# A hybrid encoder step on one core: the prologue's modulation pieces, squares and engine orders rearranged

## What is computed

```python
sh1, sc1, gt1, sh2, sc2, gt2 = adaln(cs[grp], w_ada[i], b_ada[i])   # silu(c) @ w_ada + b_ada, split in six
h = modulate(rms_norm(x, norm_mix[i]), sh1, sc1)                    # norm * (1 + scale) + shift
mix, S_fin = gla_mixer(h, S0, gla_w_in[j], ...)                     # begins with h @ gla_w_in
```

## Time and profile before

| | us |
|---|---|
| median of 3 executions (lowest, highest) | 1425.83 (1424.13, 1426.85) |
| the profiled execution | 1425.07 |
| its span in the trace | 1423.1 |
| TensorE busy | 1383.6 (97%) |
| VectorE, ScalarE, GpSimd busy | 950.0, 653.9, 88.4 |

### The profile page before, as it was taken

The page is one execution under the profiler, slowest core; times in us unless marked ns, Lnnn a source line. Parts: engine busy times, 40 slices in busy tenths (PEclk is TensorE's granted clock), DMA queues, the critical chain, the costliest instruction groups (busy, mean ns, idle before and its releaser), DMA issues.

```text
span 1423.1 us, 26319 instructions
## 1 busy us (share of the span) xinstructions
PE 1383.6 (97%) x10896; PEld 1304.1 (92%) x10896; DVE 950.0 (67%) x1591; ACT 653.9 (46%) x1454; POOL 88.4 (6%) x149
## 2 busy tenths in 40 slices
PE   8999999999999999999899999999899999999999
PEld 6878887989999999999898787879799999999999
DVE  4678677368988788778665556475888654554544
ACT  4543344256554254252465555643565552552530
POOL 0000000110000000000300000000300000000000
PEclk9999999999999999999999999999999999999999
DMA  9543533234444544535433233212334223223222
GB/s 383 221 156 138 184 131 105 67 119 161 157 155 143 175 150 148 175 119 166 155 132 104 77 104 132 80 38 83 119 119 149 90 67 112 89 67 112 75 64 106
DMA packets 37582, 182.42 MB, mean 128 GB/s; under 512 B 4246, under 2 KB 6422, under 8 KB 26072
## 3 DMA queue, kind: packets, MB, share of 16 engines
q1 hardware_dynamic: 22552, 126.98, 25.5%
q0 software_dynamic: 14912, 53.78, 10.9%
HBM read 172.82 MB, written 7.91 MB: 127 GB/s over the span
## 4 chain that ended last, share of the span: by engine, by line
PE 87%; DVE 6%; ACT 3%; issue 2%; DMA 1%; POOL 0%; SPq 0%; DVEq 0%; ACTq 0%; POOLq 0%
PE ps L603 26%; PE ps L605 26%; PE ps L604 26%; ACT w_hi L1087 1%; DVE w_lo L1551 1%; PE ps L989 1%; DMA a_pro<-in_ada_w 1%; PE ps L1030 1%; PE ps L948 1%; DVE h_lo L1636 1%; DVE oT L1583 1%; PE ps L1008 1%; DVE sq L1623 1%; DVE xT L1708 1%; PE ps L641 1%
## 5 line engine op out<-in xcount | busy, mean ns | idle before, releaser
L603 PE MATMUL ps<-h_hi,w_hi 128*128 128x272 f32 x2080 | 610.7, 294 | 16.4 <-DVE h_lo L1636 8.6
L605 PE MATMUL ps<-h_hi,w_lo 128*128 128x272 f32 x2080 | 604.3, 291 | 0.0
L604 PE MATMUL ps<-h_lo,w_hi 128*128 128x272 f32 x2080 | 600.9, 289 | 0.0
L603 PEld LDWEIGHTS ps<-h_hi,w_hi 128*128 128x128 f32 x2080 | 394.3, 190 | 29.6 <-DVE h_lo L1636 11.2
L604 PEld LDWEIGHTS ps<-h_lo,w_hi 128*128 128x128 f32 x2080 | 394.8, 190 | 1.2 <-issue 1.0
L605 PEld LDWEIGHTS ps<-h_hi,w_lo 128*128 128x128 f32 x2080 | 393.7, 189 | 0.0
L1087 ACT CAST w_hi<-w_raw 128x2048 fp32r<-128x2048 f32 (+2 forms) x109 | 188.4, 1728 | 197.8 <-PE ps L605 173.0
L1551 DVE TENSOR_TENSOR w_lo<-w_raw,w_hi 128x2048 fp32r<-128x2048 f32 (+2 forms) x109 | 226.8, 2081 | 74.3 <-ACT w_hi L1087 73.9
L603 PE MATMUL ps<-act_hi,w_hi 128*128 128x272 f32 (+1 forms) x704 | 203.6, 289 | 1.0 <-DVE w_lo L1551 1.0
L604 PE MATMUL ps<-act_lo,w_hi 128*128 128x272 f32 (+1 forms) x704 | 203.8, 290 | 0.0
L605 PE MATMUL ps<-act_hi,w_lo 128*128 128x272 f32 (+1 forms) x704 | 203.2, 289 | 0.0
(11 more groups left out here) (260 smaller groups left out, 1628.5 us busy)
## 6 DMA issues: line engine op xcount, KB each, us to landing
w_raw<-in_wst SPq DMA_DIRECT2D x73, 1024.0 KB, 5.0
a_raw<-in_ada_r POOLq DMA_DIRECT2D x56, 512.5 KB, 4.3
w_raw<-in_wst SPq DMA_DIRECT2D x28, 768.0 KB, 4.4
a_raw<-in_ada_g POOLq DMA_DIRECT2D x24, 512.0 KB, 3.6
a_pro<-in_ada_w SPq DMA_DIRECT2D x8, 1024.0 KB, 18.1
v_raw<-in_wst SPq DMA_DIRECT2D x8, 1024.0 KB, 8.0
w_raw<-in_wst SPq DMA_DIRECT2D x8, 512.0 KB, 3.6
xT<-in_xT SPq DMA_DIRECT2D x4, 544.0 KB, 6.3
```

Source lines behind the costliest of these rows:

```text
L603: mm(out, lhs_hi, rhs_hi, start=first, stop=False)
L604: mm(out, lhs_hi, rhs_lo, start=False, stop=False)
L605: return mm(out, lhs_lo, rhs_hi, start=False, stop=last)
```

## The change

Pieces: piece i now holds the shift and the scale of feature tile i alone, 128 columns each. Loads: only 149 of the 677 columns of `vec` and 130 of the 516 of `cst` come first, the rest behind block 2; piece 0 comes ahead of block 0, which is loaded, and split, in two halves. Squares: eight buffers (five new ones, `sq`, `acc`), so ScalarE doesn't wait; VectorE adds them in four pairs, and TensorE adds up the four pair sums in PSUM with four `column_sums`. Orders: TensorE, ScalarE and VectorE handle one tile at a time. VectorE calls `gain_of(i)` (bias add and gain), `scaled(i)`, `modulated_lo(i - 1)`; TensorE calls `ada_sel(i)` as listed. The diff, without the declarations of semaphores and without context at the ends of hunks:

```diff
--- before.py
+++ after.py
@@ -48,7 +48,7 @@
-ADA_ORDER = [(0, 4 * (i % 2) + i // 2) for i in range(8)] + [(0, b) for b in range(8, NADA)] + [(1, b) for b in range(NADA)]
+ADA_ORDER = [(0, b) for b in range(8)] + [(0, b) for b in range(8, NADA)] + [(1, b) for b in range(NADA)]
@@ -61,17 +61,19 @@
-for _name, _k in [("c", 2 * KT), ("norm_g", 4 * KT), ("b_ada", DEPTH * 6 * KT), ("conv", 6 * DEPTH * 2 * FT),
-                  ("gla_g", 2), ("d_gain", 1), ("q_gain", 1), ("k_gain", 1)]:
+for _name, _k in [("c", 2 * KT), ("norm_g", 4 * KT), ("b_ada", DEPTH * 6 * KT), ("gla_g", 2), ("d_gain", 1), ("q_gain", 1), ("k_gain", 1),
+                  ("conv", 6 * DEPTH * 2 * FT)]:
     VEC[_name] = (_n, _k)
     _n += _k
 NVEC = _n
+VEC_NOW = VEC["conv"][0]
 CST = {}
 _n = 0
-for _name, _k in [("ident", P), ("cmask", P), ("sel", 2), ("bones", P), ("selm", 2 * TS), ("fold", TS), ("smask", TS), ("isc0", 1), ("isc1", 1)]:
+for _name, _k in [("ident", P), ("sel", 2), ("cmask", P), ("bones", P), ("selm", 2 * TS), ("fold", TS), ("smask", TS), ("isc0", 1), ("isc1", 1)]:
     CST[_name] = (_n, _k)
     _n += _k
 NCST = _n
+CST_NOW = CST["cmask"][0]
@@ -187,7 +189,7 @@
-acc_at = lambda which, m, half: piece_count(KT - 1, ACC_PIECES, which, m, half)
+acc_at = lambda which, m, half: piece_count(KT // 2, ACC_PIECES, which, m, half)
@@ -286,6 +288,7 @@
+        sq_pro = sb("sq_pro", [P, 5, T], c=pro)
@@ -379,9 +382,14 @@
+        x_squares = [sq_pro[:, i, :] for i in range(5)] + [sq[:, 0, :], sq[:, 1, :], acc[:, :]]
+        ada_pairs = lambda ap: ap[:, 0, 0:2 * KT].rearrange("p (t k) g -> p t k g", t=2)
+        first_half, second_half = slice(0, KT * BC // 2), slice(KT * BC // 2, KT * BC)
...
@@ -445,8 +453,7 @@
-                l, b = ADA_ORDER[i]
-                sp.dma_start(a_pro[:, i, :, :], A["ada_w"][l, b].rearrange("p (k c) -> p k c", c=BC)).then_inc(pro_in[i], 16)
+                sp.dma_start(a_pro[:, i, :, :], A["ada_p"][i].rearrange("p (k c) -> p k c", c=BC)).then_inc(pro_in[i], 16)
@@ -459,23 +466,24 @@
-            sp.dma_start(vec[:, :], A["vec"]).then_inc(vec_in, 16)
-            sp.dma_start(cst[:, :], A["cst"]).then_inc(cst_in, 16)
+            sp.dma_start(vec[:, 0:VEC_NOW], A["vec"][:, 0:VEC_NOW]).then_inc(vec_in, 16)
+            sp.dma_start(cst[:, 0:CST_NOW], A["cst"][:, 0:CST_NOW]).then_inc(cst_in, 16)
             for i in range(4):
                 sp.dma_start(xT[:, 2 * i:2 * i + 2, :], A["xT"][:, 2 * i:2 * i + 2, :]).then_inc(x_in[i], 16)
-            load(0)
+            ada_load(0)
+            sp.dma_start(w_raw[:, 0, first_half], A["wst"][0, :, first_half]).then_inc(first_in, 16)
             sp.dma_start(aw[:, :, :], A["aw"]).then_inc(aw_in, 16)
-            ada_load(0)
             ada_load(1)
-            ada_load(2)
-            ada_load(3)
-            for i in range(4, 8):
+            sp.dma_start(w_raw[:, 0, second_half], A["wst"][0, :, second_half]).then_inc(w_in[0], 16)
+            for i in range(2, NPRO):
                 ada_load(i)
             load(1)
             for r in (0, HD):
                 sp.dma_start(w_alpha[r:r + 2 * RANK + 1, :], A["w_alpha"]).then_inc(gla_in, 16)
             sp.dma_start(scan0[:, :], A["scan0"]).then_inc(gla_in, 16)
             load(2)
+            sp.dma_start(cst[:, CST_NOW:NCST], A["cst"][:, CST_NOW:NCST]).then_inc(masks_in, 16)
+            sp.dma_start(vec[:, VEC_NOW:NVEC], A["vec"][:, VEC_NOW:NVEC]).then_inc(conv_in, 16)
@@ -667,9 +675,14 @@
-                    pe.wait_ge(w_lo_ok, n + 1)
+                    if n:
+                        pe.wait_ge(w_lo_ok, n + 1)
+                    else:
+                        pe.wait_ge(first_low_ok, 1)
                     for u in block_units(name):
                         bank_free(u)
+                elif n == 0 and ks[0] == KT // 2:
+                    pe.wait_ge(w_lo_ok, 1)
@@ -754,32 +767,37 @@
-            pe.wait_ge(acc_ok, KT - 1)
-            column_sums(acc, True, True).then_inc(sums_ok, 1)
-            pe.wait_ge(c_ok, 1)
-            ada_mm(0)
+            for i in range(4):
+                if i == 2:
+                    pe.wait_ge(c_ok, 1)
+                    ada_mm(0)
+                pe.wait_ge(acc_ok, i + 1)
+                ins = column_sums(x_squares[2 * i], i == 0, i == 3)
+            ins.then_inc(sums_ok, 1)
+            ada_sel(0)
             ada_mm(1)
-            ada_sel(0)
             ada_sel(1)
             ada_mm(2)
             keep_warm(WARM_TILE, 3)
             first_tile(0)
+            ada_sel(2)
             ada_mm(3)
-            ada_sel(2)
+            first_tile(1)
             ada_sel(3)
-            first_tile(1)
             ada_mm(4)
             ada_mm(5)
             first_tile(2)
             ada_sel(4)
             ada_sel(5)
             ada_mm(6)
-            ada_mm(7)
             first_tile(3)
             ada_sel(6)
+            ada_mm(7)
+            first_tile(4)
             ada_sel(7)
-            for k in range(4, KT):
+            for k in range(5, KT):
                 first_tile(k)
+            pe.wait_ge(masks_in, 16)
@@ -1096,9 +1114,7 @@
-                    if m >= 2:
-                        act.wait_ge(acc_ok, max(1, m - 2))
-                A_(sq[:, m % 2, c], xT[:, m, c], ACT.Square).then_inc(sq_ok, 1)
+                A_(sq[:, m % 2, c] if which else x_squares[m], xT[:, m, c], ACT.Square).then_inc(sq_ok, 1)
@@ -1187,25 +1203,30 @@
-            split(0)
+            part(0)
+            act.wait_ge(first_in, 16)
+            act.copy(w_hi[:, 0, first_half], w_raw[:, 0, first_half]).then_inc(first_hi_ok, 1)
             act.wait_ge(aw_in, 16)
             act.copy(aw_hl[:, :, 0:RANK], aw[:, :, :]).then_inc(aw_hi_ok, 1)
             root(0)
-            part(0)
             part(1)
             modulated(0, 0)
             part(2)
             modulated(0, 1)
+            act.wait_ge(w_in[0], 16)
+            act.copy(w_hi[:, 0, second_half], w_raw[:, 0, second_half]).then_inc(w_hi_ok, 1)
             part(3)
             modulated(0, 2)
             part(4)
             part(5)
             modulated(0, 3)
             part(6)
+            modulated(0, 4)
             part(7)
-            for k in range(4, KT):
-                modulated(0, k)
+            modulated(0, 5)
             split(1)
+            modulated(0, 6)
+            modulated(0, 7)
@@ -1355,6 +1376,7 @@
+                act.wait_ge(conv_in, 16)
@@ -1551,12 +1573,10 @@
-                l, b = ADA_ORDER[i]
                 dve.wait_ge(ada_sel_ok, i + 1)
-                t = slice(2 * b, 2 * b + 2)
                 _, _, bank, c = RIDER_AT[i]
-                TT(ada[:, l, t, :], ps[:, bank, c:c + 4].rearrange("p (t g) -> p t g", g=2),
-                   b_ada[:, l, t, None].broadcast_to([P, 2, 2]), ALU.add).then_inc(ada_ok, 1)
+                bias = b_ada[:, 0, 0:2 * KT].rearrange("p (t k) -> p t k", t=2)[:, :, i, None].broadcast_to([P, 2, 2])
+                TT(ada_pairs(ada)[:, :, i, :], ps[:, bank, c:c + 4].rearrange("p (t g) -> p t g", g=2), bias, ALU.add).then_inc(ada_ok, 1)
@@ -1729,26 +1749,47 @@
-            for m in range(1, KT):
-                dve.wait_ge(sq_ok, m + 1)
-                if m > 1:
-                    dve.wait_ge(acc_ok, m - 1)
-                TT(acc[:, :], sq[:, 0, :] if m == 1 else acc[:, :], sq[:, m % 2, :], ALU.add).then_inc(acc_ok, 1)
-            low(0)
+            for i in range(4):
+                dve.wait_ge(sq_ok, 2 * i + 2)
+                TT(x_squares[2 * i], x_squares[2 * i], x_squares[2 * i + 1], ALU.add).then_inc(acc_ok, 1)
+            dve.wait_ge(first_hi_ok, 1)
+            TT(w_lo[:, 0, first_half], w_raw[:, 0, first_half], f32(w_hi[:, 0, first_half]), ALU.subtract).then_inc(first_low_ok, 1)
             dve.wait_ge(aw_hi_ok, 1)
             TT(aw_hl[:, :, RANK:2 * RANK], aw[:, :, :], f32(aw_hl[:, :, 0:RANK]), ALU.subtract).then_inc(aw_ok, 1)
-            for b in range(4):
-                ada_add(2 * b)
-                ada_add(2 * b + 1)
-                make_gain(0, (2 * b, 2 * b + 2), 2 * b + 2)
-                if b == 0:
-                    dve.wait_ge(rstd_ok, 1)
-                rms = (acc[:, 0:TP], acc[:, TP:T])
-                scaled(0, 2 * b, rms)
-                scaled(0, 2 * b + 1, rms)
-                modulated_lo(0, 2 * b)
-                modulated_lo(0, 2 * b + 1)
+            rms = (acc[:, 0:TP], acc[:, TP:T])
+
+            def gain_of(i):
+                ada_add(i)
+                make_gain(0, (i, i + 1), i + 1)
+
+            gain_of(0)
+            dve.wait_ge(rstd_ok, 1)
+            scaled(0, 0, rms)
+            gain_of(1)
+            scaled(0, 1, rms)
+            modulated_lo(0, 0)
+            gain_of(2)
+            scaled(0, 2, rms)
+            modulated_lo(0, 1)
+            dve.wait_ge(w_hi_ok, 1)
+            TT(w_lo[:, 0, second_half], w_raw[:, 0, second_half], f32(w_hi[:, 0, second_half]), ALU.subtract).then_inc(w_lo_ok, 1)
+            gain_of(3)
+            scaled(0, 3, rms)
```

(25 more changed lines are left out.)

## The result

| | before | after |
|---|---|---|
| median of 4 executions (lowest, highest), us | 1425.84 (1424.13, 1426.85) | 1435.73 (1432.43, 1436.75) |
| profiled execution, us | 1425.07 | 1435.50 |
| its span | 1423.1 | 1433.5 |

The account below looks back on a forecast made before the run. TensorE was taken to bound the kernel, through the start of its dense work and its interruptions. 1425.07 + 7.6 (longer prologue) + 1.6 (clock) = 1434.3; allowing for medians, the forecast was 1434.5 us, range 1428.5 to 1441.

Parts of the forecast that it names:

- Tile 0: First prologue tile on TensorE: starts at 22.93, 1.11 us earlier, 3.25 us after piece 2 lands at 19.68.
- The clock term: TensorE after the new waits of 2.3 and 2.0 us: one low-clock spell of 3.3 us, costing 1.6 us.
- The ring: Prologue tiles 1 to 5: each waits for selection, gain, scaling and low part in turn, 4.86 us a round.
- Block 1's low half: VectorE work ahead of scaling 7: tile 6 starts 4.02 us after tile 5, 2.0 of it idle.
- Loads: Load queue at the front: 457 KB less ahead of piece 2, which lands 1.11 us earlier, at 19.68.
- A (dense row): Prologue tiles stay back to back and only the first tile's earlier start counts: 1424.0 us; chance 0.14.
- B (a fall at each wait): Clock falls at each of the six prologue waits, six spells of 1.6 us: 1442.3 us; chance 0.12.
- C (no fall): TensorE's clock does not fall at the new prologue waits: 1432.7 us; chance 0.22.
- D (given back later): Later TensorE waits for VectorE (2.57 and 1.81) vanish, giving back 4.4 us: 1429.9 us; chance 0.06.
- Sum: Whole kernel: 1425.07 plus 7.6 for the prologue plus 1.6 for the clock, 1434.3 us.

Follow-up runs that it names:

- squares_only: The kernel before with the squares part alone (eight buffers, four pair sums, four column-sum calls); 1429.11 us, ratio 1.0022.
- probe_ring: The changed kernel with one more VectorE copy of 544 columns between gain and scaling of tiles 2 to 6; 1439.9 us (two executions).
- dve_lo_first: The changed kernel with VectorE's order alone altered: each tile's low part ahead of the next gain, block 1's low half last; 1427.52 us, ratio 1.0014.
- sel_ahead: The changed kernel with TensorE's order alone altered: each selection and its product one tile earlier; 1427.25 us, ratio 1.0011.
- the probe: Five extra VectorE copies of 0.36 us, added to the changed kernel (1439.9 us) and to dve_lo_first (1428.50 us).
- loads_only: The kernel before with vec and cst cut to their early columns, the rest loaded behind block 2; 1423.32 us, ratio 0.9991.
- fill_wait: The changed kernel with nine more unused identity matmuls ahead of product 2; 1434.45 us, ratio 1.0062.
- dense_filled: The changed kernel with both engines' orders altered, no twenty warming matmuls, and unused matmuls in the idle stretches ahead of tile 0; 1421.72 us, ratio 0.9974.
- dense_warm: The changed kernel with TensorE's and VectorE's orders both altered and the warming matmuls kept; 1426.73 us, ratio 1.0019.

## Why the prediction was right, step by step

**Tile 0, forecast 22.93, measured 24.97.** This is the term that was mis-sized. Piece 2 came at 20.09 (19.68), and from there to the tile it took 4.88 and not 3.25 us, since the warming matmuls ran at the lower clock. Product 2's 0.41 and the warming's 1.63 make up the 2.04 by which tile 0 was late. The clock term itself was 1.6 us and 3.88 - 2.26 = 1.6 came, but I had placed the spell behind tile 5, after the waits of 2.3 and 2.0, and no fall followed these. It came ahead of tile 0, behind idle stretches (0.49 and 1.59) which I had worked out as free: I asked of the squares part only when the root is ready, and not how long TensorE idles afterwards. squares_only shows what that omission can cost, tile 0 3.7 us late, 2.8 of them given back once its waits are filled. Why the clock fell in after is not shown: probe_ring has after's program on TensorE up to tile 0 and the same waits ahead of product 2 (0.49 and 1.60, and 0.85 and 0.45 before them), and its clock stayed up until tile 1.

**The ring, forecast a start of tile 5 24.75 us after tile 0.** Measured 49.69 - 24.97 = 24.72. The rounds were 4.81, 4.84, 5.34, 4.93 and 4.80 for 4.86, 4.86, 5.31, 4.86 and 4.86. The waits sum to 8.0 where I had 9.0; TensorE's busy time includes the end of the pipeline, which the working by starts does not. Five of the six, 6.4 us, are the ring's; the last, 1.58, is block 1's low half. dve_lo_first and sel_ahead open the ring from either side and end the prologue 6.65 and 6.57 us earlier; the probe adds its length to each wait inside and nothing to the tiles' distance outside. That the ring is the cause of these 6.4 us is shown, not argued. The 8.2 and 8.5 us by the medians are more than it accounts for.

**Block 1's low half, forecast 4.02 from tile 5 to 6.** Measured 3.85; taking it away ended the prologue 1.64 earlier.

**Loads.** 1.11 us foretold for piece 2; loads_only has 0.9. In after only 0.7 of it were seen (20.79 to 20.09), possibly for the reason that made the loads late in squares_only, which stays open.

**Rivals.** A (dense row) was refuted by the six waits. B (a fall at each wait) was refuted by the stretch 25 to 58 at full clock; in probe_ring, with waits 0.36 longer, two spells fell among the six. The Trainium skill, "TensorE: Matmul & The Clock Gate", section "HAM oscillation — how this bites in real kernels", tells of waits between bursts that throttle each burst. Its waits are some 3 to 5 us, longer than the 0.4 to 2.2 us of this train, which did not do so; the two don't contradict each other, and the prediction should not have taken the page for a case of rival B. C (no fall) is refuted by 21.6 to 25. D (given back later) did not occur: the shift at the end of the prologue, 9.46, was 9.46 at the next block, and grew.

**Sum.** 1434.3 was worked out against the profiled execution, which gave 1435.5; the prologue had +9.2 forecast, +9.46 measured. The clock's share of it, one sixth, had the right size in the wrong place, which is luck; the ring's share is not.

## What to carry to other kernels

Where two engines work through hand-written lists, look for a ring and draw it for one item: if A's step for item i + 1 stands behind its work on item i, and B puts the finishing of item i behind its start of i + 1, each item pays the whole round trip, here 2.8 us less the 0.4 to 2.3 of work beneath it. A change of order on either engine alone opens it. And when an early phase gets faster, ask what the engine with the gated clock does in the time that it wins: an earlier end that turns work into waiting can cost more than it gives.

## What the runs showed of the clock that was not expected

The length of a single wait does not say whether the clock falls. It fell after 0.49 and 1.59 with little work between them (after), after 2.12 and 1.32 (squares_only), already at 18.8 after 0.46 and 0.49 (fill_wait) and on tile 1 in probe_ring, behind a wait of 1.6, and again at 52.6 there, shortly after one of 2.58. It did not fall ahead of tile 0 in probe_ring, behind the waits of 0.49 and 1.60 after which it fell in after; nor did it fall in 25 to 58 us of after with waits of 0.36 to 2.22, each between 2 us or more of dense matmuls. With ten pairs of unused matmuls spread over all idle stretches it stayed up in dense_filled; with nine pairs in the last stretch alone it fell in fill_wait. This is one profiled execution of each, and the executions of one kernel differ by up to 9.9 us (1422.20 to 1432.14 for squares_only, 1424.46 to 1431.73 for dense_warm). after and probe_ring show that a spell's place is not the same in each, so that the filling kept the clock up is likely and not shown.
